# The rests of the block-product weights go from GpSimd to VectorE, the sums of the raw weights the other way, with one bank pair fewer and larger VectorE instructions

## The reference, cut to what matters

```python
h = rmsnorm(x, pre_mlp_norm)                                  # 512 x 1024
f = jnp.square(jax.nn.relu(h @ w_mlp_in)) @ w_mlp_out         # 512 x 4096, then 512 x 1024
x = x + rmsnorm(f, post_mlp_norm)
```

## Time and profile before

| | us |
|---|---|
| median of 3 runs | 1773.3 (1772.96 to 1774.67) |
| the profiled execution, its own time | 1773.85 |
| its span | 1772.0 |
| TensorE (PE) busy | 1750.1 (99%) |
| VectorE (DVE) busy | 935.4 (53%) |
| ScalarE (ACT) busy | 877.3 (50%) |
| GpSimd (POOL) busy | 868.3 (49%) |

### The profile page before, as it was taken

The page is one execution under the profiler, slowest core; times in us unless marked ns, Lnnn a source line. Parts: engine busy times, 40 slices in busy tenths (PEclk is TensorE's granted clock), DMA queues, the critical chain, the costliest instruction groups (busy, mean ns, idle before and its releaser), DMA issues.

```text
span 1772.0 us, 26114 instructions
## 1 busy us (share of the span) xinstructions
PE 1750.1 (99%) x8768; PEld 1469.8 (83%) x8768; DVE 935.4 (53%) x1574; ACT 877.3 (50%) x1867; POOL 868.3 (49%) x634
## 2 busy tenths in 40 slices
PE   8999999999999999999999999999999999999998
PEld 7888888888888888888878788888888888898887
DVE  5587787878305555245494857260163312355763
ACT  4655556555425665334544444353534442367662
POOL 4553445465553132454477768645464444542322
PEclk9999999999999999999999999999999999999999
DMA  5731221221133121332514232324232223322211
GB/s 184 136 103 60 71 66 64 63 68 60 60 107 119 44 88 49 131 109 93 191 47 143 70 121 96 125 78 178 71 118 84 83 94 97 95 76 64 66 49 60
DMA packets 46810, 163.13 MB, mean 92 GB/s; under 512 B 4827, under 2 KB 7259, under 8 KB 46460
## 3 DMA queue, kind: packets, MB, share of 16 engines
q1 hardware_dynamic: 39744, 144.72, 25.2%
q10 hardware_dynamic: 6972, 17.16, 3.9%
HBM read 153.47 MB, written 8.39 MB: 91 GB/s over the span
## 4 chain that ended last, share of the span: by engine, by line
PE 89%; DVE 6%; issue 2%; ACT 1%; POOL 1%; DMA 0%; DVEq 0%; ACTq 0%; POOLq 0%
PE main L319 59%; PE main L347 7%; PE aux L2106 4%; PE aux L828 3%; PE main L2042 2%; PE aux L813 2%; PE aux L677 1%; PE aux L669 1%; PE aux L690 1%; PE aux L795 1%; PE aux L794 1%; PE aux L391 1%; PE aux L642 1%; PE aux L645 1%; PE aux L2149 1%
## 5 line engine op out<-in xcount | busy, mean ns | idle before, releaser
L282 POOL TENSOR_TENSOR w_lo<-raw,w_hi 128x512 fp32r<-128x512 f32 x456 | 618.9, 1367 | 750.8 <-ACT w_hi L278 746.0
L278 ACT ACTIVATE w_hi<-raw 128x512 fp32r<-128x512 f32 x438 | 272.3, 629 | 540.7 <-PE main L319 513.8
L319 PE MATMUL main<-a_hi,w_hi 128*128 128x512 f32 x704 | 286.3, 407 | 0.1
L319 PE MATMUL main<-a_hi,w_lo 128*128 128x512 f32 x704 | 275.1, 391 | 0.0
L319 PE MATMUL main<-a_lo,w_hi 128*128 128x512 f32 x704 | 274.3, 390 | 0.0
L319 PE MATMUL main<-w_hi,a_hi 128*128 128x512 f32 x608 | 248.0, 408 | 0.7 <-DVE gt L2440 0.7
L319 PE MATMUL main<-w_hi,a_lo 128*128 128x512 f32 x608 | 237.5, 391 | 0.0
L319 PE MATMUL main<-w_lo,a_hi 128*128 128x512 f32 x608 | 237.0, 390 | 0.0
L319 PEld LDWEIGHTS main<-a_hi,w_lo 128*128 128x128 f32 x704 | 132.1, 188 | 28.6
L319 PEld LDWEIGHTS main<-a_hi,w_hi 128*128 128x128 f32 x704 | 132.4, 188 | 24.9 <-issue 1.1
L319 PEld LDWEIGHTS main<-a_lo,w_hi 128*128 128x128 f32 x704 | 132.7, 188 | 24.2
(11 more groups left out here) (393 smaller groups left out, 3607.3 us busy)
## 6 DMA issues: line engine op xcount, KB each, us to landing
raw<-w_stream_in SPq DMA_DIRECT2D x240, 512.0 KB, 3.6
raw_x<-w_pairs_in SPq DMA_DIRECT2D x12, 512.0 KB, 3.6
raw<-w_pairs_in SPq DMA_DIRECT2D x12, 512.0 KB, 3.6
x_res<-x_in ACTq DMA_DIRECT2D x8, 512.0 KB, 5.1
rel_rows<-rel_row ACTq DMA_DIRECT2D x1, 4096.0 KB, 44.3
bias<-rel_rows ACTq DMA_DIRECT2D x2, 1536.0 KB, 8.0
x_rows<-x_res SPq DMA_DIRECT2D x4, 512.0 KB, 6.1
x_res<-x_rows SPq DMA_DIRECT2D x4, 512.0 KB, 3.3
```

Of the source, the lines that this page charges most:

```text
L278: eng.activation(w_hi[:, k, :], raw[:, k, :], ACT.Copy).then_inc(hi_done, 1)
L282: eng.tensor_tensor(w_lo[:, k, :], raw[:, k, :], w_hi[:, k, :].bitcast(F32), ALU.subtract).then_inc(lo_done, 1)
L319: mm = eng.matmul(mb[m][:, :], lhs, rhs, start=(first and k == 0 and n == 0), stop=(last and k == KT - 1 and n == 2))
```

## The change

In each chunk:

- VectorE makes the 28 rests `pair_lo`, GpSimd the eight raw sums `w_sum3`, `w_sum2`, `w_sum4`, `w_sum1` and nothing else until rest 27 is made.
- Product 1 uses BANK_Z, so there are two bank pairs; the wait for the `mb` banks goes; product 3 waits until product 1 has been taken (14c + 4).
- The feature sums are one instruction of 4 x 256 in place of four of 256. `set_lo` is one instruction for two tiles of 512 (for set 4, one for four of 256).
- VectorE's list is written anew: the rests stand in groups of four before each take, and `sum3` of the next chunk stands after the take of product 4.

```diff
-        BANK_X, BANK_Y, BANK_Z = (ab[0], ab[1]), (mb[0], mb[1]), (ab[2], ab[3])
+        BANK_X, BANK_Z = (ab[0], ab[1]), (ab[2], ab[3])
...
+        def w_sum2(eng, c, h):
+            eng.wait_ge(pair_sum, 8 * c + SUM3 + h + 1)
+            eng.wait_ge(lo_done, 8 * P_PAIR[c] + 2 * h + 2)
+            a = raw_x[:, 2 * h:2 * h + 2, :]
+            eng.tensor_tensor(a, a, raw[:, 2 * h:2 * h + 2, :], ALU.add).then_inc(pair_sum, 1)
...
 (GpSimd)
-                for t in range(28):
-                    pair_lo(pool, c, t)
+                for h in range(2):
+                    w_sum3(pool, c, h)
+                for h in range(2):
+                    w_sum2(pool, c, h)
+                for h in range(2):
+                    w_sum4(pool, c, h)
+                for h in range(2):
+                    w_sum1(pool, c, h)
+                pool.wait_ge(lo_done, 8 * P_PAIR[c] + 32)
...
 (TensorE)
-                        if j == 1 and kk == 0:
-                            pe.wait_ge(bank_free, 4 * (O_MLP + 2 * c + 2) + q + 1)
...
-                pair_product(c, 1, 2, 0, BANK_Y, 14 * c - 10, True)
+                pair_product(c, 1, 2, 0, BANK_Z, 14 * c - 2, True)
                 pair_product(c, 2, 3, 1, BANK_X, 14 * c + 2)
-                pair_product(c, 3, 3, 0, BANK_Z, 14 * c - 2, True)
+                pair_product(c, 3, 3, 0, BANK_Z, 14 * c + 4, True)
...
 (VectorE)
+            def sum2(c):
+                dve.wait_ge(f_sq, 8 * c + 8)
+                dve.wait_ge(set_ready[0], 4 * c + 4)
+                dve.tensor_tensor(f_even[:, :, right], f_odd[:, :, right], f_even[:, :, right], ALU.subtract).then_inc(s2_done, 4)
...
+                sum2(c)
+                sum1(c)
+                set_lo(2, c, 0, 2, f_odd)
+                set_lo(2, c, 2, 2, f_odd)
+                rests(0, 1)
+                set_lo(3, c, 0, 2, f_even)
+                rests(1, 2)
+                set_lo(3, c, 2, 2, f_even)
+                rests(2, 3)
+                sum4(c)
+                rests(3, 7)
+                set_lo(4, c, 0, 4, f_odd[:, :, left])
+                rests(7, 8)
                 relu_row(2 * c + 2, f_even)
+                rests(8, 12)
                 take_product(c, 0, BANK_X, 0, 0, c > 0)
+                rests(12, 16)
+                take_product(c, 1, BANK_Z, 0, 0, True)
+                rests(16, 20)
+                take_product(c, 2, BANK_X, 0, 1, c > 0)
+                rests(20, 24)
+                take_product(c, 3, BANK_Z, 1, 1, c > 0)
+                rests(24, 28)
+                take_product(c, 4, BANK_X, 1, 1, True)
+                if c < 2:
+                    sum3(c + 1)
+                take_product(c, 5, BANK_Z, 0, 1, True)
+                (set_lo(1) of the next chunk, or out_lo(6) in the last)
                 take_product(c, 6, BANK_X, 1, 0, c > 0)
```

More of the change, by code:

```diff
@@ L1248, in pair_lo, with w_sum3, w_sum4, w_sum1 @@
                               ALU.subtract).then_inc(lo_done, 5 if t == 27 else 1)
+        def w_sum3(eng, c, h):
+            eng.wait_ge(pair_landed[4 + h], 16 * (c + 1))
+            eng.wait_ge(pair_landed[6 + h], 16 * (c + 1))
+            b, dd = raw[:, 2 * h:2 * h + 2, :], raw[:, 4 + 2 * h:6 + 2 * h, :]
+            eng.tensor_tensor(b, dd, b, ALU.subtract).then_inc(pair_sum, 1)
+        def w_sum2(eng, c, h):
[3 more added lines that the diff above has]
+            eng.tensor_tensor(a, a, raw[:, 2 * h:2 * h + 2, :], ALU.add).then_inc(pair_sum, 1)
+        def w_sum4(eng, c, h):
+            eng.wait_ge(pair_sum, 8 * c + SUM2 + h + 1)
+            eng.wait_ge(lo_done, 8 * P_PAIR[c] + 4 + 2 * h + 2)
+            cc = raw_x[:, 4 + 2 * h:6 + 2 * h, :]
+            eng.tensor_tensor(cc, cc, raw_x[:, 2 * h:2 * h + 2, :], ALU.subtract).then_inc(pair_sum, 1)
+        def w_sum1(eng, c, h):
+            eng.wait_ge(pair_sum, 8 * c + SUM4 + h + 1)
+            eng.wait_ge(lo_done, 8 * P_PAIR[c] + 8 + 2 * h + 2)
+            a = raw_x[:, 2 * h:2 * h + 2, :]
+            eng.tensor_tensor(a, raw[:, 4 + 2 * h:6 + 2 * h, :], a, ALU.subtract).then_inc(pair_sum, 1)
         block = ctx.enter_context(nc.Block())
@@ L2460, in relu_row, with set_lo @@
                     dve.scalar_tensor_tensor(f[:, m, :], mb[m][:, :], 0.0, root_row[:, :], ALU.max, ALU.mult).then_inc(bank_free, 1)
-            def set_lo(part, count, kk, f):
-                dve.wait_ge(set_hi[part - 1], count)
+            def set_lo(part, c, k0, kn, f):
+                dve.wait_ge(set_hi[part - 1], 4 * c + k0 + kn)
                 s_hi, s_lo = (set1, set2, set3, set4)[part - 1]
-                dve.tensor_tensor(s_lo[:, kk, :], f, s_hi[:, kk, :].bitcast(F32), ALU.subtract).then_inc(set_ready[part - 1], 1)
+                ks = slice(k0, k0 + kn)
+                dve.tensor_tensor(s_lo[:, ks, :], f[:, ks], s_hi[:, ks, :].bitcast(F32), ALU.subtract).then_inc(set_ready[part - 1], kn)
@@ L2467, in _ @@
             left, right = slice(0, 2 * P), slice(2 * P, 4 * P)
[L2469 to L2516, removed]
+            def sum3(c):
+                dve.wait_ge(f_sq, 8 * c + 4)
+                dve.tensor_tensor(f_even[:, :, right], f_even[:, :, left], f_even[:, :, right], ALU.subtract).then_inc(s3_done, 4)
@@ new lines, in sum2, with sum1, sum4 @@
+            def sum2(c):
+                dve.wait_ge(f_sq, 8 * c + 8)
+                dve.wait_ge(set_ready[0], 4 * c + 4)
+                dve.tensor_tensor(f_even[:, :, right], f_odd[:, :, right], f_even[:, :, right], ALU.subtract).then_inc(s2_done, 4)
+            def sum1(c):
+                dve.wait_ge(s2_done, 4 * c + 4)
+                dve.tensor_tensor(f_even[:, :, left], f_even[:, :, right], f_even[:, :, left], ALU.add).then_inc(s1_done, 4)
+            def sum4(c):
+                dve.wait_ge(set_ready[1], 4 * c + 4)
+                dve.tensor_tensor(f_odd[:, :, left], f_odd[:, :, left], f_even[:, :, right], ALU.subtract).then_inc(s4_done, 4)
@@ L2538, in _ @@
             relu_row(0, f_even)
[L2539 to L2542, removed]
+            sum3(0)
+            set_lo(1, 0, 0, 2, f_even)
+            set_lo(1, 0, 2, 2, f_even)
             for c in range(3):
@@ L2546, in _, with rests @@
                 relu_row(2 * c + 1, f_odd)
[L2547 to L2564, removed]
+                sum2(c)
+                sum1(c)
+                set_lo(2, c, 0, 2, f_odd)
+                set_lo(2, c, 2, 2, f_odd)
+                def rests(t0, t1):
+                    for t in range(t0, t1):
+                        pair_lo(dve, c, t)
+                dve.wait_ge(lo_done, 8 * P_PAIR[c])
+                rests(0, 1)
[7 more added lines that the diff above has]
+                rests(7, 8)
                 dve.wait_ge(s4_done, 4 * c + 4)
@@ L2567, in _ @@
                 relu_row(2 * c + 2, f_even)
-                w_sum4(c, 1)
+                rests(8, 12)
                 take_product(c, 0, BANK_X, 0, 0, c > 0)
-                w_sum1(c, 0)
-                w_sum1(c, 1)
-                if c < 2:
[L2573 to L2579, removed]
+                rests(12, 16)
[6 more added lines that the diff above has]
+                take_product(c, 4, BANK_X, 1, 1, True)
+                if c < 2:
+                    sum3(c + 1)
+                take_product(c, 5, BANK_Z, 0, 1, True)
+                for k in (0, 2):
                     if c < 2:
-                        set_lo(1, 4 * c + 4 + kk + 1, kk, f_even[:, kk, :])
+                        set_lo(1, c + 1, k, 2, f_even)
                     else:
-                        out_lo(6, kk)
-                take_product(c, 5, BANK_Z, 0, 1, True)
+                        out_lo(6, k)
+                        out_lo(6, k + 1)
                 take_product(c, 6, BANK_X, 1, 0, c > 0)
```

## The result

The changed kernel takes 1784.0 us (median of 4, 1782.6 to 1785.9) against 1773.6 before: ratio 1.0060, 95% interval 1.0048 to 1.0072. The forecast was 1775.3, with a range up to 1779.5. It is slower by 10.5 us, outside the range.

A forecast was written before the change was run, and what follows sets the result against it. PE's list bounds the kernel (busy 1750.1 of 1772.0 us). Lost 3 x 2.5 = 7.5, won 5.5: +2.0 on the profiled 1773.85 gives 1775.85, less 0.55 over the median: 1775.3, range 1767.3 to 1779.5.

The forecast's parts named there:

- At most 5.5 us to be won: PE's waits at products 1 and 4 in the three chunks, idle plus slow restart, were all that could be won.
- The waits of products 1 and 4 go: Product 1's wait for relu_row goes, returning 2.8 us; product 4's for take 2 goes if VectorE is in time, 2.7 us.
- A new wait: product 3 now needs take 1: Take 1 stands behind rests 12 to 15, so product 3 starts late: 2.5 us taken for each of three chunks.
- The walk: Step-by-step timing of GpSimd and VectorE in the first chunk, ending with take 1 at 921.05 and product 3 at 921.2.
- its weak term: The stall's size: 0.1 us more or less in one long operation is 0.7 a chunk and 2.1 in all.
- its own sign of being wrong: Wrong if a sum's price is off by over 0.2 us, or another order at the shared port frees VectorE earlier.
- rival B's smaller case: Batched 4 x 256 sums at 1.34 put 0.8 us more on each chunk's chain: +4.4, 1777.7.
- rival A's 1.90: GpSimd's sums take 1.90 us each and don't hold VectorE up enough; no PE wait in the chunks, 1767.8; chance 0.26.
- The engines exclude each other at SBUF: VectorE instructions with two SBUF operands that meet a GpSimd sum end 0.55 (512) or 1.08 us (1024) after it.
- The estimate of 2.25 for a sum: GpSimd sum of 1024, from the skill's 4497 ns for 2048 float32 elements; the prediction itself took 2.36.
- B: Take 1 is later still, so product 3 stalls longer; up to 1780.7 with 2.58 for each sum; chance 0.27.
- C: VectorE itself becomes the bound over the whole chunk, take 4 or the next panel waiting; 1781; chance 0.02.

The follow-up runs named there:

- `sum3` later: The kernel before with one move: sum3 of the next chunk stands behind take 2 in VectorE's list; 1770.8 us, ratio 0.9987.
- the bank alone: The kernel before with product 1 in BANK_Z, its mb wait gone, and sum3 of the next chunk behind take 2, nothing batched; 1770.1 us, ratio 0.9982.
- Take 0 first: The changed kernel with VectorE taking product 0 right behind relu_row, ahead of rests 8 to 11; 1789.0 us, ratio 1.0088.
- the short sums: The changed kernel with GpSimd's eight sums working on only 4 columns of each tile, order and waits kept; 1768.2 us, ratio 0.9972.
- both takes first: The changed kernel with take 0 ahead of rests 8 to 11 and take 1 ahead of rests 12 to 15; 1771.9 us, ratio 0.9994.
- everything on VectorE: The changed kernel with the eight sums also on VectorE, among the rests, and takes 0 and 1 a little earlier in its list; 1768.0 us, ratio 0.9972.
- the sums in halves: The changed kernel with each of GpSimd's eight sums as two instructions of 512 instead of one of 1024; 1780.2 us, ratio 1.0041.

## Why the prediction was wrong

- **At most 5.5 us to be won:** right. The four runs in which no product starts late lie at 1767.6 to 1768.8, 4.8 to 6.0 us under the kernel before measured beside them.
- **The waits of products 1 and 4 go:** right. `sum3` later alone gives product 4's part as forecast (1770.8). Product 1's 2.8 us stand in no run by themselves: the bank alone has the move of `sum3` too and is only 0.7 us faster than it, since products 2 and 3 start late there.
- **"A new wait: product 3 now needs take 1":** this is the step that failed. It looked for new waits among those whose number the diff changes, and product 2's (BANK_X, 14c + 2) is not among them. But take 0, for which product 2 waits, was moved behind rests 8 to 11. The walk had the time of it, 916.3, and never set it against product 2's due time of 913.3, though it did so for tiles 8, 11 and 12 and for takes 1, 2 and 4. That check alone gives 916.3 + 0.15 - 913.26 = 3.2 us, 3.3 with the restart, in each chunk; product 3 is then due at 922.0, behind take 1, and adds nothing: 3 x 3.3 - 5.5 = +4.4 on the profiled 1773.85, less its 0.55 over the median: 1777.7. Take 0 first removed the wait at product 2, which shows it. The prediction called the size its weak term, "not the mechanism"; it was the other way round, and its own sign of being wrong, a sum's price off by over 0.2 us, did not come (2.40 against 2.36). That rival B's smaller case gives 1777.7 as well is chance: its wait is at product 3.
- **The walk's sizes:** good. A sum took 2.40 (2.36 taken, and rival A's 1.90 is out); a rest held by one 2.88 (2.9), a `set_lo` 3.41 (3.4); take 0 ended at 917.04 (916.3), take 1 at 921.90 (921.05). Of the 0.7 at take 0, 0.3 is there when `sum2` ends (886.71, in the walk 886.39), as the first sum waited for D's first half until 883.22 (882.95), and 0.4 after the two `set_lo` 2 (892.52, in the walk 892.1), though the second sum waited for its half until 887.43 (886.4). The rest came in steps of 0.1 or less. That makes product 2 start 3.9 late in the first chunk; the others had 3.5. Against the 3.2 of the check that is 1.3 us more in all.
- **A term left out:** no part of the sum had the clock. Two of the three waits were followed by a stretch at 1.2 GHz, 1.7 us each, 3.4 in all. With them the profiled execution adds up: 1773.85 + 14.3 - 5.5 = 1782.65, measured 1782.57. The median lies 1.4 above that, which stays inferred as said above.
- **The engines exclude each other at SBUF:** right by the rows (a rest that met a sum ended 0.56 after it, 0.55 in the walk), and what it costs is shown by the short sums (1768.2) and by both takes first against everything on VectorE (1771.9 against 1768.0). The rule that the prediction took from the Trainium skill (SBUF — State Buffer, Who interferes with whom) holds in these runs: 2.88 against 0.68. The estimate of 2.25 for a sum, worked out from the Trainium skill (GPSIMD Engine Reference, section 3.1), is 0.15 under the 2.40 measured.
- **The rivals:** B's sign was right and its mechanism near: take 1 later still. The wait was at a take that no rival named. A is out by the rows (2.40, 2.88 and 3.41), C by the short sums.
- **The range** took in the unknown prices, but not that a due time could have been left unchecked, nor the clock.

## What to carry to other kernels

When a list is written anew, go through every wait of the engine that sets the end, not only those that the diff edits: a moved instruction is the far end of waits whose lines stand unchanged. Work given to GpSimd isn't free for a VectorE whose instructions read two operands from SBUF: a sum cost 2.4 on one engine and held the other for up to 2.2, against 1.2 in VectorE's own list, so the load by busy time did not tell which split was faster. And a wait of PE of some microseconds can cost its clock on top.

## What the runs showed of the hardware

- A GpSimd subtraction of 128 x 1024 float32 with two full operands takes 2.40 us; the rows before had 1.90 for 1024 with one operand repeated, 1.27 for 512 and 0.74 for 256.
- The clock after a wait: in the changed kernel it fell to 1.2 GHz after idle times of 3.78 and 3.31 us and not after 3.34; with the sums in halves after 2.44 and one of 2.16 and not after the other 2.16, which a second wait of 0.36 followed; with take 0 first after 4.45, 3.90 and 3.90, and the low stretch was longer. In the chunks of these runs it stayed at 2.4 GHz after every wait of 1.33 and less. A fall cost 1.6 to 1.7 us in the changed kernel and with the sums in halves, and 2.4 in the window shown with take 0 first. The steps between matmuls of 512 columns were 0.427 and 0.227 us at the two levels. The Trainium skill (TensorE: Matmul & The Clock Gate, Part 1) has 0.427 and 0.216 for them; the first agrees, the second is 0.011 more here.
